# Weight products of two projections placed between the units of two attentions

## The reference, cut to what matters

```python
aq, ak, av, bq, bk, bv, cq, cf, cb, ci, cg, gates = features(h_lat, w_in[l], qn_b[l], kn_b[l], rope)
...
ya = window_attn(aq, ak, av, cak, cav, sink_a[l])
yb = global_attn(bq, bk, bv, cbk, cbv)
...
up = jnp.einsum('blnw,nwd->blnd', ys, w_branch)
g = jax.nn.sigmoid(gates.reshape(B_, L, N_BRANCH, -1))
return jnp.sum(g * up, axis=2) @ w_out
```

## Time and profile before

| | us |
|---|---|
| median of three runs (3064.24 to 3068.4) | 3065.93 |
| the profiled execution, its own time | 3068.42 |
| its span, first to last instruction | 3066.6 |
| TensorE busy, share of the span | 2910.8, 95% |
| VectorE busy | 1550.9, 51% |
| ScalarE busy | 1206.6, 39% |
| GpSimd busy | 333.3, 11% |

### The profile page before, as it was taken

The page is one execution under the profiler, slowest core; times in us unless marked ns, Lnnn a source line. Parts: engine busy times, 40 slices in busy tenths (PEclk is TensorE's granted clock), DMA queues, the critical chain, the costliest instruction groups (busy, mean ns, idle before and its releaser), DMA issues. The chain is left out here.

```text
span 3066.6 us, 39504 instructions
## 1 busy us (share of the span) xinstructions
PE 2910.8 (95%) x14988; PEld 2310.3 (75%) x14988; DVE 1550.9 (51%) x2177; ACT 1206.6 (39%) x1797; POOL 333.3 (11%) x286
## 2 busy tenths in 40 slices
PE   7999987999999999899999999999899999999998
PEld 2889765688878888686687878888686777778886
DVE  2467246555544443447753454443458663544434
ACT  3642424532233332334643343332435652333333
POOL 0020004500001110001200121100102102111100
PEclk8999999999999999999999999999999999999999
DMA  6100210035422222121032112232120131122222
GB/s 242 69 28 1 90 55 1 1 130 182 179 73 97 96 96 96 65 83 42 29 109 97 56 69 96 96 105 96 56 83 15 56 133 47 66 87 98 98 104 94
DMA packets 43555, 254.09 MB, mean 83 GB/s; under 512 B 4608, under 2 KB 6784, under 8 KB 15872
## 3 DMA queue, kind: packets, MB, share of 16 engines
q1 hardware_dynamic: 43392, 251.87, 23.1%
HBM read 249.75 MB, written 2.10 MB: 82 GB/s over the span
## 5 line engine op out<-in xcount | busy, mean ns | idle before, releaser
L250 DVE TENSOR_TENSOR ring_lo<-ring,ring_hi 128x2048 fp32r<-128x2048 f32 x201 | 460.8, 2292 | 797.4 <-ACT ring_hi L243 797.1
L243 ACT ACTIVATE ring_hi<-ring 128x2048 fp32r<-128x2048 f32 x201 | 383.8, 1910 | 467.0 <-PE bank L301 345.1
L301 PE MATMUL bank<-h_hi,ring_hi 128*128 128x512 f32 x1360 | 539.8, 397 | 7.7 <-PEq L349 4.1
L301 PE MATMUL bank<-h_hi,ring_lo 128*128 128x512 f32 x1360 | 530.3, 390 | 0.0
L1544 PE MATMUL bank<-h_hi,ring_hi 128*128 128x512 f32 x960 | 374.2, 390 | 5.7 <-DVE ring_lo L250 5.7
L1548 PE MATMUL bank<-h_hi,ring_lo 128*128 128x512 f32 x960 | 373.5, 389 | 0.0
L1547 PE MATMUL bank<-h_lo,ring_hi 128*128 128x512 f32 x960 | 373.4, 389 | 0.0
L301 PEld LDWEIGHTS bank<-h_hi,ring_hi 128*128 128x128 f32 x1360 | 256.0, 188 | 66.6 <-issue 10.2
L301 PEld LDWEIGHTS bank<-h_hi,ring_lo 128*128 128x128 f32 x1360 | 255.8, 188 | 53.9
L301 PE MATMUL bank<-h_lo,ring_hi 128*128 128x512 f32 x624 | 243.3, 390 | 0.0
L1544 PEld LDWEIGHTS bank<-h_hi,ring_hi 128*128 128x128 f32 x960 | 180.2, 188 | 45.5 <-issue 5.5
(11 more groups left out here) (444 smaller groups left out, 4978.8 us busy)
## 6 DMA issues: line engine op xcount, KB each, us to landing
ring<-in_stream SPq DMA_DIRECT2D x209, 1024.0 KB, 4.8
mod_w<-in_stream SPq DMA_DIRECT2D x64, 256.0 KB, 5.0
xT<-in_xT SPq DMA_DIRECT2D x2, 2048.0 KB, 15.2
const<-in_const SPq DMA_DIRECT2D x1, 2306.5 KB, 15.5
par<-in_par SPq DMA_DIRECT2D x3, 696.0 KB, 3.9
memT<-in_memT SPq DMA_DIRECT2D x2, 1024.0 KB, 4.9
out<-xT SPq DMA_DIRECT2D x1, 2048.0 KB, 6.2
ctxT<-in_ctxT SPq DMA_DIRECT2D x1, 1024.0 KB, 4.8
```

What stands on the lines that cost most here:

```text
L243: nc.scalar.activation(self.slab_hi(slab + j), self.slab(slab + j), ACT.Copy).then_inc(slab_rounded, 1)
L250: nc.vector.tensor_tensor(lower, self.slab(slab + j), self.slab_hi(slab + j).bitcast(F32), ALU.subtract)\
L301: ins = nc.tensor.matmul(out, lhsT, rhs, start=start and w is w_hi and x is x_hi, stop=stop and w is w_lo)
```

## The change

Seventy-two weight blocks leave their stages and are made in the attentions, by a class `Beside` that puts some blocks (two in most units) between the transposes of a unit, into bank 7.

- B now comes before A. B makes A's four query tiles (32 blocks, formerly in front) with their rotation, and the first gate tile of the merge; A makes the next four gate tiles. List `upto` says how many blocks are done by each unit, and `turns` and `rounds` at which units a query tile is rotated and a slab is rounded and halved: three slabs in B, two in A.
- Transposes go four at a time into banks 4, 5 and again 4 (the third group after the first has been copied; B's units and A's units of 5 key blocks have one). VectorE copies the first and third group, ScalarE the second. The values go to bank 6 alone.
- VectorE's inverses(u+1) stand after the first copy of unit u and ahead of its last.
- A's masks and sinks of both heads are one operation each.
- In front `gate_scan` goes to GpSimd, `key_logs` stands ahead of the reading of the first `cg` tile (tile 14), and A's query tiles and their rotations are gone: 18 tiles.
- The merge has 19 gate tiles and 24 branch tiles. It starts with gate 5 and six branch products; five sigmoids of the gates made before stand at its start on ScalarE. Its first slabs are put together from pieces: 15 loads in place of 5.

The core of the diff follows; of removed lines only some are shown, the functions before stand above.

```diff
+GATE_BLOCKS = lambda g: 12 * g
+BRANCH_BLOCKS = lambda g: 12 * g + 8
+MERGE_PIECES = (
+    ((0, GATE_BLOCKS(0), 8), (8, GATE_BLOCKS(1), 4), (12, GATE_BLOCKS(1) + 4, 4)),
+    ((0, GATE_BLOCKS(2), 8), (8, GATE_BLOCKS(3), 8)),
+    ((0, GATE_BLOCKS(4), 8), (8, GATE_BLOCKS(5), 4), (12, GATE_BLOCKS(5) + 4, 4)),
+    ((0, BRANCH_BLOCKS(1), 4), (4, BRANCH_BLOCKS(4), 4), (8, BRANCH_BLOCKS(2), 4), (12, BRANCH_BLOCKS(5), 4)),
+    ((0, BRANCH_BLOCKS(0), 4), (4, BRANCH_BLOCKS(3), 4), (8, GATE_BLOCKS(6), 8)))
...
+                    elif layer[0] is None and 0 <= g - FRONT < 8:
+                        src = stream[g + APART + (3 if g - FRONT < 2 else 2 if g - FRONT < 6 else -6)]
+                    elif layer[0] is None and 0 <= g - MERGE < len(MERGE_PIECES):
+                        *others, (to, of, n) = MERGE_PIECES[g - MERGE]
+                        for o_to, o_of, o_n in others:
+                            o_slab, o_at = divmod(o_of, SLAB)
+                            sp.dma_start(dst[:, o_to * P:(o_to + o_n) * P], stream[MERGE + APART + o_slab][:, o_at * P:(o_at + o_n) * P])\
+                                .then_inc(pieces_loaded[g - MERGE], 16)
+                        dst = dst[:, to * P:(to + n) * P]
+                        src = stream[MERGE + APART + of // SLAB][:, of % SLAB * P:(of % SLAB + n) * P]
...
+        class Beside:
...
+            def products(self, pe, u):
+                while self.blocks < self.upto[u]:
+                    m, k = divmod(self.blocks, KT)
+                    if k == 0 and m > 0:
+                        if m <= len(self.turns):
+                            pe.wait_ge(self.by_sin.sem, self.by_sin.at(m))
+                        else:
+                            pe.wait_ge(self.tile_read.sem, self.tile_read.at(m))
+                    last = ws.mm(pe, self.tiles[m]["at"] + k, 1, bank[:, 7, :], (h_hi[:, k, :], h_lo[:, k, :]), True, k == 0, k == KT - 1)
+                    if k == KT - 1:
+                        last.then_inc(self.tile_done.sem, 1)
+                    self.blocks += 1
+            def turn(self, pe, u):
+                if u in self.turns:
+                    m = self.turns.index(u)
+                    pe.wait_ge(self.tile_read.sem, self.tile_read.at(m + 1))
+                    nc.tensor.matmul(bank[:, 7, :], con("rot1"), self.tiles[m]["out"], start=True, stop=True).then_inc(self.turned.sem, 1)
+            def scalar(self, act, u):
+                while self.read < self.upto[u] // KT:
+                    tile = self.tiles[self.read]
+                    act.wait_ge(self.tile_done.sem, self.tile_done.at(self.read + 1))
+                    nc.scalar.activation(tile["out"], bank[:, 7, :], ACT.Copy, scale=tile["scale"]).then_inc(self.tile_read.sem, 1)
+                    self.read += 1
+                if u in self.rounds:
+                    ws.round_to(act, self.rounds[u], ws.limit)
+            def sines(self, dve, u):
+                if u in self.turns:
+                    m = self.turns.index(u)
+                    dve.wait_ge(self.turned.sem, self.turned.at(m + 1))
+                    nc.vector.tensor_tensor(self.spare, bank[:, 7, :], self.table[:, 1, :], ALU.mult).then_inc(self.by_sin.sem, 1)
+            def vector(self, dve, u):
+                if u - 1 in self.turns:
+                    out = self.tiles[self.turns.index(u - 1)]["out"]
+                    nc.vector.tensor_tensor(out, out, self.table[:, 0, :], ALU.mult)
+                    dve.drain()
+                    nc.vector.tensor_tensor(out, out, self.spare, ALU.add)
+                if u in self.rounds:
+                    ws.halve_to(dve, self.rounds[u], ws.limit)
...
+                def transposes(u, b):
+                    if b >= len(groups(u)):
+                        return
+                    _, first, end = groups(u)[b]
+                    if b == 2:
+                        pe.wait_ge(probs_out[0].sem, probs_out[0].at(u + 1))
+                    elif u > 0:
+                        pe.wait_ge(probs_out[b].sem, probs_out[b].at(u))
+                        if b == 0 and thirds[u]:
+                            pe.wait_ge(probs_out[2].sem, probs_out[2].at(thirds[u]))
+                    for x in range(first, end):
+                        g, j = divmod(x, units[u]["keys"])
+                        if j == 0 or x == first:
+                            pe.wait_ge(probs_ready.sem, probs_ready.at(2 * u + g + 1))
+                        last = nc.tensor.transpose(bank[:, (4, 5, 4)[b], (x - first) * P:(x - first + 1) * P],
+                                                   probs[:, u % 2, g, j * P:(j + 1) * P], con("ident"))
+                    last.then_inc(turned[b].sem, 1)
...
                 scores(0)
+                beside.products(pe, 0)
+                for u in range(N):
+                    if u + 1 < N:
+                        scores(u + 1)
+                    if u > 0:
                         values(u - 1)
+                    beside.turn(pe, u)
+                    transposes(u, 0)
+                    transposes(u, 1)
+                    beside.products(pe, u + 1)
+                    transposes(u, 2)
+                values(N - 1)
...
+                logs_with_exps(act)
+                beside.scalar(act, 0)
                 exps(0)
                 for u in range(N):
+                    if u + 1 < N:
+                        exps(u + 1)
+                    _, first, end = groups(u)[1]
+                    act.wait_ge(turned[1].sem, turned[1].at(u + 1))
+                    nc.scalar.activation(probsT[:, u % 2, first * P:end * P], bank[:, 5, 0:(end - first) * P], ACT.Copy)\
+                        .then_inc(probs_out[1].sem, 1)
+                    beside.scalar(act, u + 1)
...
+                    if unit["masks"]:
+                        at, n, mask = unit["masks"]
+                        cols = S[:, :, at:at + n * 256].rearrange("p g (m n) -> p g m n", n=256)[:, :, :, 0:P] if n == 2 else S[:, :, at:at + P]
+                        nc.vector.tensor_tensor(cols, cols, mask, ALU.add)
+                    if sink:
+                        nc.vector.tensor_copy(S[:, :, w - 1:w], sink(u // TB))
+                        dve.drain()
...
+                def copy(u, b):
+                    if b < len(groups(u)):
+                        _, first, end = groups(u)[b]
+                        dve.wait_ge(turned[b].sem, turned[b].at(thirds[u + 1] if b == 2 else u + 1))
+                        nc.vector.tensor_copy(probsT[:, u % 2, first * P:end * P], bank[:, 4, 0:(end - first) * P]).then_inc(probs_out[b].sem, 1)
...
+                inverses(0)
+                for u in range(N):
+                    if u + 1 < N:
+                        maxima(u + 1)
+                    if u % TB == 0 and u:
+                        turn_out(u // TB - 1)
+                    beside.sines(dve, u)
+                    copy(u, 0)
+                    if u + 1 < N:
+                        inverses(u + 1)
+                    copy(u, 2)
+                    beside.vector(dve, u + 1)
...
-                def gate_scan(dve, n):
-                    outs.wait(dve, CG + n)
-                    nc.vector.tensor_tensor(yc[:, n, :], yc[:, n, :], cg[:, n, :], ALU.mult)
+                def gate_scan(pool):
+                    for n in range(C_HEADS):
+                        outs.wait(pool, CG + n)
+                        pool.wait_ge(row_normed.sem, row_normed.at(n + 1))
+                        nc.gpsimd.tensor_tensor(yc[:, n, :], yc[:, n, :], cg[:, n, :], ALU.mult)
...
-                tiles += [("act", T, weights_still(F0 + (8 + n) * KT, KT, h), act_copy(qkA[:, n, :], scale=HD ** -0.5)) for n in range(4)]
-                tiles += [("act", T, weights_still(F0 + (12 + n) * KT, KT, h), act_copy(cg[:, n, :], ACT.Silu)) for n in range(C_HEADS)]
-                QA, CG = 14, 18
+                tiles += [("act", T, weights_still(F0 + (8 + n) * KT, KT, h), act_copy(cg[:, n, :], ACT.Silu)) for n in range(C_HEADS)]
...
-                        ("act", 7): lambda act: log_rows(act, QUERY[:2]), ("act", 9): key_squares, ("act", 15): key_logs,
+                        ("act", 7): lambda act: log_rows(act, QUERY[:2]), ("act", 9): key_squares, ("act", 14): key_logs,
...
+            queries = [dict(at=(FRONT + 6) * SLAB + n * KT, out=qkA[:, n, :], scale=HD ** -0.5) for n in range(4)]
+            first_gates = [dict(at=MERGE * SLAB + g * KT, out=gates[:, g, :], scale=1.0) for g in range(GATES_FIRST)]
+            upto = [7, 8, 10, 12, 14, 16, 18, 20, 22, 24, 26, 28, 30, 32, 34, 37, 40]
+            beside = Beside(queries + first_gates[:1], upto, (1, 5, 9, 13), {1: FRONT + 7, 8: MERGE, 15: MERGE + 1}, axial, rope_spare[:, :])
+            attend("B", 1, False, qkB, kB, vab[:, :, P:2 * P], work, beside)
+            upto = [7, 8, 10, 12, 14, 16, 18, 20, 22, 24, 26, 28, 30, 32, 32, 32, 32]
+            beside = Beside(first_gates[1:], upto, (), {3: MERGE + 2, 11: MERGE + 3})
```

(57 more changed lines are left out.)

182 lines of the change are left out of this document (72 added, 110 removed).

## The result

The changed kernel took 3043.2 us (median of four runs, 3040.65 to 3045.11) beside 3066.94 for the kernel before on the same chip: a ratio of 0.9924, 95% interval 0.9911 to 0.9936. The forecast was 3043.5. The profiled execution took 3040.65 with a span of 3038.9.

The account below looks back on a forecast made before the run. TensorE was taken to bound merge, front and B, with some room in A. Front -30.8, B +31.4, A +3.7 and merge -26.7 sum to -22.4, taking 3065.93 to 3043.5 us; range 3031 to 3057 for 8 in 10.

Parts of the forecast that it names:

- the term of the logarithms: Front: the first rotation's 3.14 us wait goes because the logarithms now stand ahead of tile 14's read-out, -3.1 us.
- the clock behind it: Front: time lost as at a lower clock after the first rotation's wait goes too, -1.6 us.
- One sine wait: Front: one of two waits for VectorE's sine product goes with the rotations, -0.9 us; the other stays.
- The steady unit: B: a unit where nothing stalls takes 5.92 us from scores to scores, with TensorE idle for little.
- The interval at unit 1: B: VectorE's halving waits for ScalarE's rounding, maxima and sine product queue behind; scores go from 11.1 to 20.95 us.
- the halving at unit 8: B: a halving that follows rounding overruns the room in its unit by 0.6 us.
- the two allowances of 1.0: B: +1.0 us for half-clock time after unit 1's stall, +1.0 for VectorE and GpSimd holding each other up.
- the rival's +12: Rival: GpSimd and VectorE exclude each other in full, thirteen operations 1.0 late, none hidden, 3055.5 us; chance 0.07.
- a pair of heads: A: a pair of heads (four units) with its weight blocks takes 19.3 us on TensorE.
- the allowance of 0.5: Merge: rounding and splitting of slabs are hidden behind branch products by about 1 us; 0.5 us added.
- Room for blocks in B: Rival: TensorE finds room in B, 33 blocks cost nothing, another -22.4 us, 3021; chance 0.05.
- The third transposes' wait: Rival, both attentions: third transposes reuse bank 4, wait for VectorE's first copy and make the kernel slower; chance 0.07.

Follow-up runs that it names:

- run 8: The changed kernel with the logarithms of B's keys again behind the reading of tile 14 in front: 3048.45 us (single run).
- run 2: As run 1, but in B the third group of transposes goes to bank 7 from unit 2 on: 3043.34 us (single run).
- run 10: The changed kernel with GpSimd multiplying only the first 128 columns of each head's probabilities in both attentions: 3042.3 us (single run).
- the change again: The changed kernel, unaltered, measured once more on the same chip: 3042.58 us, ratio 0.9918 to the kernel before.
- run 1: The changed kernel with A's four query tiles and rotations back in front, B keeping only the first gate tile: 3053.83 us.
- run 9: The changed kernel with VectorE's inverses of the next unit behind the last copy, as before the change: 3056.44 us.
- runs 5 and 6: Against the changed kernel: 5, B's three halvings one unit after rounding, 3040.53 us; 6, only B's first two and A's so, A's blocks rearranged, 3038.57 us.

## Why the prediction was right

- **Front.** -30.9 for -30.8; run 8 shows the term of the logarithms and the clock behind it: 5.1 for 4.7. One sine wait of 0.87 stayed, as said. GpSimd's last gate product took 1.26 for the 1.04 read from another product.
- **The total.** The mechanism held, but that the median comes within 0.3 us of the forecast is luck: the stages moved by 21.2, the medians by 23.7, and executions of the change differ by 4.5.
- **B, the sum.** +31.0 for +31.4, and run 2 shows why: against a B whose units take 4.59, as before the change, the moved work costs in full on balance. The steady unit (5.81 for 5.92), the rotation (1.07 for 0.94) and the end (15.95 for 16.0) had nearly their size. The interval at unit 1 was 10.53 for 9.85, the unit behind it 6.41 for 5.92, and the halving at unit 8 cost 1.8 for 0.6: the rounding that it waits for was on the way there as at unit 1. These misses of some 2.3 us were met by the two allowances of 1.0 and by seven plain units that were 0.1 shorter each.
- **B, the clock and the port.** +1.0 each was put down. The first stall's window ran at a granted clock of 0.90 over 16.9 us, and this cost some 1.7: from the block behind the stall to the next scores 3.02 for 1.90, in the unit behind 6.41 for 5.81. The port's price is run 10, a single run in which GpSimd is also done sooner: 1.04. VectorE and GpSimd do hold each other up in full: 1.39 for 0.69 and 3.00 for 2.29 on the one, 4.86 for 2.89 on the other. The Trainium skill (SBUF — State Buffer, Who interferes with whom) says so, and the rows of the change agree with it; but of some 3.7 us of lengthened instructions in B only 1.0 is in the path, so the rival's +12 didn't come.
- **A.** +5.9 for +3.7, of which 1.6 is that execution's clock; the change again gives +4.25. The halvings cost the 1.6 each that were forecast, a pair of heads 19.5 for 19.3. How much of A's cover is room and how much its shorter chain stays open.
- **Merge.** -27.2 for -26.7; the allowance of 0.5 wasn't needed, and loads moved 178 GB/s for the 193 expected.
- **The rivals.** Room for blocks in B, against the old order, is excluded by run 2. The third transposes' wait is real (run 1, 0.40 a unit), but two blocks of 1.36 stand ahead of it and hide it: its mechanism was right and its cover was there.
- **What it didn't price.** The order of the inverses is worth 13 us here (run 9). The prediction took steady units to be bound by TensorE, which holds only with it.

What stays open: the first gap of B took 8.0 to 8.1 in runs 1, 2 and 8, at a granted clock of 0.79, and 6.5 in the eight others with all its blocks, at 1.00 in the change. Why the clock was lower in these three is not shown: TensorE waits 2.3 us just ahead of it in all of them and in the change alike. In run 8 a wait of 3.14 lies 27 us ahead; in runs 1 and 2 front has no such wait.

## What to carry to other kernels

Work put between the units of a full TensorE costs its own time there too; it pays only in gaps and in units whose chain is longer than TensorE's sum, so add up both for each kind of unit. To ask what a change's piece costs, take it out of both orders: taken out of the new order alone, the blocks seemed 30% cheaper than they were (18.4 us for 26.45), because another wait appeared. In B a subtraction that follows a rounding belongs one unit behind it (5.3 us), and not beside GpSimd's products at the stage's end; in A, begun earlier beside them, it saved 0.15.

## What the runs showed of the hardware

- A VectorE instruction with two operands in SBUF and a GpSimd product wait for each other: 0.69 to 1.39, 2.29 to 3.00 and 3.06 us on VectorE, 2.89 to 4.86 on GpSimd; in runs 5 and 6 the delay is what was left of the other's instructions, to within 0.15.
- The granted clock of TensorE fell behind some of its waits of 1.6 to 3.4 us, and matmuls took longer for some us: scores of B 2.15 for 1.56 behind a wait of 2.56, in a window at 0.90. Behind a wait of 1.74 in A the same code ran at 0.74 in one execution (6.56) and at 1.00 in the next (4.94).
- With the same code ahead, a stage starts up to 2.8 us earlier or later from one execution to another.
